# Three joints and the end of a fused two-block kernel rearranged: attention's output, the second mixer's banks and weights, the last tile in two halves

## What is computed

```
def first_block(x, ...):
    h = x
    h = h + mamba2_mixer(rms_norm(h, g_pre[0]), ...)
    k_nope, k_rope, v = mla_shared_kv(h, ...)
    h = h + mla_mixer(rms_norm(h, g_pre[1]), k_nope, k_rope, v, ...)
    return rms_norm(h, g_final)

def second_block(x, ...):
    x = x + 0.5 * swiglu(rmsnorm(x, ffn1_norm), ...)
    x = x + hybrid_mixer(rmsnorm(x, mix_norm), ...)
    x = x + 0.5 * swiglu(rmsnorm(x, ffn2_norm), ...)
    return rmsnorm(x, final_norm)
```

## Time and profile before

| what | value |
|---|---|
| median of 3 runs | 1859.54 us (1858.78 to 1861.8) |
| the profiled execution's own time | 1858.74 us |
| its span in the profile | 1856.8 us |
| TensorE busy, share of the span | 98% |
| TensorE's share of the chain that ended last | 89% |
| VectorE busy; its share of the chain | 56%; 6% |
| ScalarE busy; its share of the chain | 39%; 2% |
| mean granted clock of TensorE | 0.995 |

### The profile page before, as it was taken

One profiled execution on the slowest core, in us unless ns is written; L12 is line 12 of the kernel. 1 busy time (PEld: TensorE's weight loads), 2 busy tenths in 40 slices (PEclk: granted clock), 3 DMA queues, 4 the chain that ended last, 5 costly groups with the idle time before them and its releaser, 6 DMA issues.

```text
span 1856.8 us, 20948 instructions
## 1 busy us (share of the span) xinstructions
PE 1812.9 (98%) x8276; PEld 1458.1 (79%) x8276; DVE 1039.2 (56%) x1486; ACT 727.0 (39%) x1195; POOL 56.8 (3%) x123
## 2 busy tenths in 40 slices
PE   7899999999999999999999999999999999999997
PEld 5677777887866678888888788888888888888885
DVE  6888886566488466444433346654444544444233
ACT  4577776334366543222232333222222433232221
POOL 3000101100210000000000000000000000000000
PEclk9999999999999999999999999999999999999998
DMA  4222122322211132333333323333323223333331
GB/s 152 71 76 69 69 80 69 102 88 84 86 46 35 35 101 91 101 92 102 93 95 97 116 83 97 92 102 94 99 91 103 91 91 102 94 99 89 104 94 54
DMA packets 47041, 163.82 MB, mean 88 GB/s; under 512 B 5216, under 2 KB 5472, under 8 KB 46944
## 3 DMA queue, kind: packets, MB, share of 16 engines
q1 hardware_dynamic: 46656, 162.29, 27.8%
q10 hardware_dynamic: 288, 0.20, 0.0%
HBM read 160.37 MB, written 2.10 MB: 87 GB/s over the span
## 4 chain that ended last, share of the span: by engine, by line
PE 89%; DVE 6%; ACT 2%; issue 1%; POOL 1%; DVEq 0%; POOLq 0%; ACTq 0%
PE pb L697 27%; PE pb L699 26%; PE pb L698 26%; PE pb L782 2%; PE pb L889 2%; PE pb L894 1%; PE pb L918 1%; DVE wl L1375 1%; PE pb L1010 1%; PE pb L1012 1%; PE pb L1011 1%; ACT wr L1070 1%; DVE XL L1393 1%; PE pb L707 0%; PE pb L1020 0%
## 5 line engine op out<-in xcount | busy, mean ns | idle before, releaser
L697 PE MATMUL pb<-XR,wr 128*128 128x512 f32 x1592 | 630.6, 396 | 19.4 <-DVE XL L1393 10.6
L698 PE MATMUL pb<-XL,wr 128*128 128x512 f32 x1592 | 622.2, 391 | 0.0
L699 PE MATMUL pb<-XR,wl 128*128 128x512 f32 x1592 | 621.9, 391 | 0.0
L1375 DVE TENSOR_TENSOR wl<-raw,wr 128x1024 fp32r<-128x1024 f32 (+1 forms) x298 | 359.6, 1207 | 366.0 <-ACT wr L1070 365.2
L1070 ACT ACTIVATE wr<-raw 128x1024 fp32r<-128x1024 f32 (+1 forms) x296 | 307.1, 1038 | 308.3 <-PE pb L699 283.3
L697 PEld LDWEIGHTS pb<-XR,wr 128*128 128x128 f32 x1592 | 300.3, 189 | 86.4 <-issue 16.1
L699 PEld LDWEIGHTS pb<-XR,wl 128*128 128x128 f32 x1592 | 300.2, 189 | 63.8
L698 PEld LDWEIGHTS pb<-XL,wr 128*128 128x128 f32 x1592 | 300.6, 189 | 60.8
L1079 ACT ACTIVATE SQ<-H 128x512 f32<-128x512 f32 x42 | 26.5, 632 | 113.8 <-DVE H L1539 61.2
L697 PE MATMUL pb<-ffn1HR,wr 128*128 128x512 f32 x176 | 68.5, 389 | 0.0
L698 PE MATMUL pb<-ffn1HL,wr 128*128 128x512 f32 x176 | 68.5, 389 | 0.0
(11 more groups left out here) (316 smaller groups left out, 2227.6 us busy)
## 6 DMA issues: line engine op xcount, KB each, us to landing
raw<-in_ffn_in SPq DMA_DIRECT2D x88, 512.0 KB, 3.5
raw<-in_mix_in SPq DMA_DIRECT2D x48, 512.0 KB, 3.5
raw<-in_ssm_in SPq DMA_DIRECT2D x41, 512.0 KB, 3.3
raw<-in_ffn_out SPq DMA_DIRECT2D x32, 512.0 KB, 3.5
raw<-in_ffn_out SPq DMA_DIRECT2D x16, 384.0 KB, 3.1
raw<-in_mla_in SPq DMA_DIRECT2D x11, 512.0 KB, 3.3
raw<-in_ssm_out_a SPq DMA_DIRECT2D x8, 512.0 KB, 3.2
raw<-in_ssm_out_b SPq DMA_DIRECT2D x8, 512.0 KB, 3.2
```

What stands on the lines that cost most here:

```text
L697: e.matmul(o, r, xr, start=first, stop=False)
L698: e.matmul(o, r, xl, start=False, stop=False)
L699: return e.matmul(o, l, xr, start=False, stop=last)
L1375: e.tensor_tensor(wl[j % NS][:, 0:width(j)], raw[j % NR][:, 0:width(j)], wr[j % NS][:, 0:width(j)].bitcast(F32), ALU.subtract).then_inc(s_ ...
```

## The change

In `latents` the spread of "ck" (placing, TensorE's side, VectorE's copy) goes from `i == 4` to `i == 5`. At the end of attention the weight split is called ahead of the squares on ScalarE, the squares and folds of the last tiles stand behind ffn1's input parts, and the ring of banks leaves out bank 0. In the second mixer the second half of "vg" gets banks 0, 1, 2, 4, gates and token mixings exchange their groups of banks, and the split of the third gate's weights is called ahead of the second gelus and of the root. ffn2's ring starts with bank 1. ffn2's last output tile is computed in two halves of 256 tokens, each with its own residual, square, sums, root (two of four columns), spread and scalings; sums and spread of the first stand in the stream of the second; the stores are halves too, those of the second half's odd tiles issued by ScalarE. The diff, without new names and numbers of sessions and with the `ck` and `vg` edits that repeat left out:

```diff
@@ banks
-        if i == 4:
+        if i == 5:
             bk.place("spread ck", 7, (s_spread, spreads["ck"] + 1), (s_rk, 1))
...
-    ring = Ring([4, 5, 6, 0, 1, 2])
+    ring = Ring([4, 5, 6, 1, 2])
     for n in range(3, 8):
         bk.place(("mo", n), ring.next(), whole("mla_out", n), (s_res, 8 + n + 1))
...
-        ring = Ring([0, 1, 2, 4, 5, 6, 7])
+        ring = Ring([0, 1, 2, 4, 5, 6, 7] if f == 0 else [1, 2, 4, 5, 6, 7, 0])
...
+        if f == 1:
+            for p in range(2):
+                bk.place(("last", p), ring.next(), (s_last, p + 1), (s_res, 40 + p))
+                b = 3 if p == 0 else ring.next()
+                bk.place(("sum", p), b, (s_sums, sums_no[f"fin{p}"]), (s_sv, taken[f"fin{p}"]))
+                bk.place(("spread", p), b, (s_spread, spreads[f"fin{p}"] + 1), (s_fin, 8 * p + 8))
...
-            bk.place(("vg", hf, i), 4 + i, whole("mix_v", 4 * hf + 3), (s_vg, 4 * hf + i + 1))
+            bk.place(("vg", hf, i), ((4, 5, 6, 7), (0, 1, 2, 4))[hf][i], whole("mix_v", 4 * hf + 3),
+                     (s_vg, 4 * hf + i + 1))
...
-    ring, mring = Ring([0, 1, 2]), Ring([4, 5, 6, 7])
+    ring, mring = Ring([5, 6, 7]), Ring([0, 1, 2, 4])
@@ SP
-        for n in range(KT):
-            w.wait_ge(s_fin, n + 1)
-            e.dma_start(out[n], H[:, n, :]).then_inc(s_out, 16)
+        for p in range(2):
+            tk = slice(256 * p, 256 * p + 256)
+            for n in range(KT):
+                if p == 0 or n % 2 == 0:
+                    w.wait_ge(s_fin, 8 * p + n + 1)
+                    e.dma_start(out[n][:, tk], H[:, n, tk]).then_inc(s_out, 16)
@@ TensorE
+        def last_sums(p):
+            o = opened(("sum", p))
+            w.wait_ge(s_fold, sq.folded["fin", 6])
+            w.wait_ge(s_lastsq, p + 1)
+            for i in (2 * p, 2 * p + 1):
+                tk = slice(128 * i, 128 * i + 128)
+                e.matmul(o[:, i:i + 1], ACC[:, tk], ones[:, 0:1], start=True, stop=False)
+                m = e.matmul(o[:, i:i + 1], TB[:, tk], ones[:, 0:1], start=False, stop=True)
+            m.then_inc(s_sums, 1)
...
+        def last_tile():
+            parts = []
+            for p in range(2):
+                o = opened(("last", p))
+                tk = slice(256 * p, 256 * p + 256)
+                for t in range(FT):
+                    if p == 1 and t == 7:
+                        last_sums(0)
+                    if p == 1 and t == 17:
+                        last_spread(0)
+                    if p == 0 and t % 8 == 0:
+                        parts.append(take("ffn2_out", 21 + t // 8))
+                    r, l = parts[t // 8]
+                    w.wait_ge(s_hlo, FT + t + 1)
+                    s = slice(128 * (t % 8), 128 * (t % 8) + 128)
+                    m = three(o[:, tk], r[:, s], l[:, s], HRS[1][:, t, tk], HLS[1][:, t, tk], t == 0, t == FT - 1)
+                m.then_inc(s_last, 1)
+            last_sums(1)
+            last_spread(1)
@@ ScalarE, attention
-            for n in range(8):
-                if n:
-                    hi()
-                if n == 7:
-                    for t in range(7):
-                        w.wait_ge(s_mlo, t + 1)
-                        x_hi(t, H[:, t, :], gain2[:, t:t + 1])
+            for n in range(6):
+                hi()
                 w.wait_ge(s_res, 8 + n + 1)
-                if n == 7:
-                    w.wait_ge(*whole("mla_out", 7))
-                    x_hi(n, H[:, n, :], gain2[:, n:n + 1])
+                square(("m1", n), H[:, n, :])
+                square(("m2", n), H[:, n, :], col("g_final", n))
+            hi()
+            w.wait_ge(s_res, 15)
+            for t in range(7):
+                w.wait_ge(s_mlo, t + 1)
+                x_hi(t, H[:, t, :], gain2[:, t:t + 1])
+            w.wait_ge(s_res, 16)
+            w.wait_ge(*whole("mla_out", 7))
+            x_hi(7, H[:, 7, :], gain2[:, 7:8])
+            for n in (6, 7):
                 square(("m1", n), H[:, n, :])
                 square(("m2", n), H[:, n, :], col("g_final", n))
@@ ScalarE, second mixer
-                for k in range(4):
+                for k in range(4 + hf):
                     hi()
...
             for j in range(10):
-                if j < 8:
+                if 1 <= j < 8:
                     hi()
@@ ScalarE, end
+        for p in range(2):
+            tk = slice(256 * p, 256 * p + 256)
+            w.wait_ge(s_res, 40 + p)
+            e.activation(TB[:, tk], H[:, 7, tk], ACT.Square).then_inc(s_lastsq, 1)
+        for n in range(1, KT, 2):
+            w.wait_ge(s_fin, 8 + n + 1)
+            e.dma_start(out[n][:, 256:512], H[:, n, 256:512]).then_inc(s_out, 16)
@@ VectorE, attention
-            for n in range(8):
-                if n:
-                    lo()
-                if n == 7:
-                    for t in range(7):
-                        x_lo(4, t, H[:, t, :], gain2[:, t:t + 1])
+            for n in range(7):
                 residual(1, n, ("mo", n))
-                if n == 7:
-                    x_lo(4, n, H[:, n, :], gain2[:, n:n + 1])
-                if n >= 2:
+                lo()
+                if 2 <= n < 6:
                     fold("m1", n - 1)
                     fold("m2", n - 1)
+            for t in range(8):
+                if t == 6:
+                    residual(1, 7, ("mo", 7))
+                x_lo(4, t, H[:, t, :], gain2[:, t:t + 1])
+            for n in (5, 6):
+                fold("m1", n)
+                fold("m2", n)
@@ VectorE, end
-        fold("fin", 7)
-        root("fin")
-        w.wait_ge(*bk.full["spread fin"])
-        for n in range(KT):
-            e.scalar_tensor_tensor(out=H[:, n, :], in0=H[:, n, :], scalar=col("final_norm", n), in1=PB[3][:, :],
-                                   op0=ALU.mult, op1=ALU.mult).then_inc(s_fin, 1)
+        fold("fin", 6)
...
+        last_residual(0)
+        last_root(0)
+        last_scale(0, range(5))
+        last_residual(1)
+        last_scale(0, range(5, KT))
+        last_root(1)
+        last_scale(1, range(KT))
```

More of the change, by code:

```diff
@@ L456, in build_in @@
     spreads = {n: i for i, n in enumerate(("x", "g0", "g1", "g2", "g3", "kv", "ck", "cq", "both", "first", "mix", "f2",
-                                           "fin"))}
+                                           "fin0", "fin1"))}
     sums_no = {n: i + 1 for i, n in enumerate(("x", "g0", "g1", "g2", "g3", "kv", "ck", "cq", "m1", "m2", "mx", "f2",
-                                               "fin"))}
-    rooted = {n: (s_root, i + 1) for i, n in enumerate(("x", "kv", "first", "both", "mx", "f2", "fin"))}
+                                               "fin0", "fin1"))}
+    rooted = {n: (s_root, i + 1) for i, n in enumerate(("x", "kv", "first", "both", "mx", "f2", "fin0", "fin1"))}
     rooted.update({n: (s_groot, i + 1) for i, n in enumerate(("g0", "g1", "g2", "g3", "ck", "cq"))})
@@ L609, in place_ffn @@
                 bk.place("spread f2", 3, (s_spread, spreads["f2"] + 1), (s_rs, 5))
-        for c in range(KT):
+        for c in range(KT if f == 0 else KT - 1):
             bk.place((name, 2, c), ring.next(), whole(name + "_out", 3 * c + 2), (s_res, 16 * (f + 1) + c + 1))
+        if f == 1:
[4 more added lines that the diff above has]
+                bk.place(("spread", p), b, (s_spread, spreads[f"fin{p}"] + 1), (s_fin, 8 * p + 8))
     place_ffn(0)
@@ L638, in build_in @@
     place_ffn(1)
-    bk.place("sum fin", 3, (s_sums, sums_no["fin"]), (s_sv, taken["fin"]))
-    bk.place("spread fin", 3, (s_spread, spreads["fin"] + 1), (s_fin, 8))
     def ffn_turn(f, j):
@@ L994, in ffn, with last_spread @@
                     m.then_inc(s_unit, 1)
+        def last_sums(p):
[7 more added lines that the diff above has]
+            m.then_inc(s_sums, 1)
+        def last_spread(p):
+            o = opened(("spread", p))
+            w.wait_ge(*rooted[f"fin{p}"])
+            for i in (2 * p, 2 * p + 1):
+                m = e.transpose(o[:, 128 * i:128 * i + 128], RN[:, i:i + 1].to_broadcast([128, 128]), ident[:, :])
+            m.then_inc(s_spread, 1)
+        def last_tile():
[17 more added lines that the diff above has]
+            last_spread(1)
         def second_mixer():
@@ L1007, in second_mixer @@
                         for i in range(4):
-                            o = opened(("vg", hf, i)) if t == 0 else PB[4 + i]
+                            o = opened(("vg", hf, i)) if t == 0 else PB[bk.bank["vg", hf, i]]
                             tk = slice(128 * i, 128 * i + 128)
@@ L1049, in _ @@
         ffn(1)
-        sums("fin")
-        spread("fin")
+        last_tile()
     @block.scalar
@@ L1301, in second_mixer @@
                     w.wait_ge(*rooted["mx"])
-                    e.activation(part, PB[4 + i][:, :], ACT.Gelu_apprx_tanh, scale=RN[:, i:i + 1]).then_inc(s_vg, 1)
+                    e.activation(part, PB[bk.bank["vg", hf, i]][:, :], ACT.Gelu_apprx_tanh,
+                                 scale=RN[:, i:i + 1]).then_inc(s_vg, 1)
```

(35 more changed lines are left out.)

20 lines of the change are left out of this document (11 added, 9 removed).

## The result

The changed kernel takes 1844.36 us (median of 4 runs, 1843.38 to 1845.1), the kernel before, with a fourth run, 1859.2 (1858.78 to 1861.8). The medians are 14.8 us apart. The ratio is 0.9918 with a 95% interval of 0.9905 to 0.9932, which makes some 15.2 us less, where 12.6 were forecast. The ratio times 1859.2 is 1843.95, just beyond the low end of the range, 1844.0. The direction and the order of size were right, the size was too small. The profiled execution took 1843.38 (span 1841.6).

What follows compares the result with a forecast made beforehand. TensorE, busy 98% of the span and 89% of the chain of waits, was taken as the bound. Five terms, 1.7 + 4.5 + 4.2 + 0.7 + 1.5 = 12.6, off 1858.74 gave 1846.1, plus 0.8 for the median 1846.9 us; range 1844 to 1852.

Steps and rivals of the forecast that it cites:

- A: Latents, spread of "ck" one tile later: the transposes' wait for POOL's root goes, minus 1.7 us.
- rival 5: The latents change gives nothing, as POOL's steps meet VectorE's only in the profiled execution: 1848.6 us; chance 0.03.
- B: Attention's output to ffn1: earlier weight splits and input parts remove TensorE's waits, minus 4.5 us, bounds 2.5 and 4.5.
- the late folds: Folds of tiles 5, 6, 7 behind XL 7: last two end about 675.7 and 676.3, just in time for ffn1's sums.
- rival 1: A stall returns, from late folds before ffn1 or the fourth gate's weights; about 4.5 us lost, 1851.4; chance 0.15.
- C: Second mixer: four waits for gelu (2.9 us) and the third gate's weight wait (1.3) go, minus 4.2, bounds 2.7 and 4.3.
- D: ffn2's first tile in bank 1: no wait for the last residual, 0.3 given back at sums; minus 0.7 us.
- E: ffn2's last tile by halves: longer matmul stream, shorter chain behind it; minus 1.5 us, bounds minus 2.4 and plus 7.7.
- rivals 3 and 4: Last tile's half matmuls: bound by 0.19 weight loads, 1856.1 us, chance 0.05; or two passes in 0.49, 1895.7, chance 0.04.
- Rival 2: The tail gives nothing: the end follows the DMAs, and doubled sums and roots eat the rest; 1848.4 us; chance 0.09.

## Why the prediction fell short

**A**, forecast 1.7, measured 1.71 in the trace; no wait came back at the next weights. The wait was 1.50 to 1.54 in all six traces of a kernel without A. Two things speak against rival 5 (that the wait is rare in the timed executions): it stands in each of these traces, and the times, mostly of executions without a kept trace, differ by 13.8, of which the traces' sum with A in it gives 13.4. No run took A out by itself. The Trainium skill (SBUF — State Buffer, Who interferes with whom) says that a VectorE instruction with two SBUF inputs contends with a GpSimd one that reads SBUF. That fits with POOL's 1.11 us, but no run here took the meeting alone away.

**B**, 4.5 against 4.5 to 4.6. The step that the forecast thought nearest to failing, the late folds, had it "just in time" at the sums, and there is indeed no wait there: by the trace the last fold into ACC ended at 672.29, 0.19 ahead of the sums. So the margin was thin, and that no stall came was in part luck. Its bound below of 2.5 and rival 1 didn't come true.

**C**, 4.2 against 4.4: banks 2.9 against 3.0, gate 1.3 against 1.3. The restart of 0.24 per interruption that I put on each idle time was good to 0.1.

**D**, 0.7 against 0.55, with the wait of 0.28 for the fold as worked out (0.3). This too is the trace alone; no run took D out.

**E** is the term of the sum that was mis-sized: minus 1.5 against minus 2.2. Up to the last scaling the steps hold to 0.2: the starts 0.120 apart, so rivals 3 and 4 are refuted; the sums to the transposes 3.33 against 3.34; the transposes to the scalings 0.70 against 0.8; eight scalings 3.22 against 3.2. The step "Before, the last VectorE instruction ended at 1854.12 and the span at 1856.8, 2.7 later; I keep 2.7" failed: it is 2.15, because the last store lands 0.50 sooner after its issue. I had named 16 transfers of half the size on two queues and still kept the time of one of full size. Rival 2 saw that the end hangs on the DMAs and took it for a loss; it was a gain.

One reading in E was wrong and did no harm. The eight sums' matmuls in 1.02, my ground for a load that does not need 0.19, were put where the clock has fallen. The mean of 0.60 was of the whole stretch from 1844 to 1857; around the sums the clock was still full (the window's columns as above):

```profile
1844.00:1846.00 2.00, 1.02 (x8) 0.97 (x8) 0.69 (x5) 0.00 (x0) 0.00 (x0) 1.00 0.01 4
```

The conclusion, a load pace well under 0.19, stands without the low clock. The Trainium skill (TensorE: Matmul & The Clock Gate, Back-to-back issue gap) gives 109 ns for 256 columns; the trace has 0.120 and decides, as it did in the forecast.

**The base** is the larger part of the miss, 1.7 of the 2.5 us between the 12.6 of the forecast and the 15.1 between the two traces. The forecast took the profiled execution, put 0.8 on it for the median, and left "1 of scatter in the runs". One stretch alone, the first heads, has two levels, some 1.4 to 1.7 us apart, that go with the clock that TensorE is granted there. In the trace of before, on which the sum stood, it was low; the profile of after had it high, and by their times so had one more of its four runs. With that held, the change is worth 13.8, of which the forecast had 12.6: 0.7 lacks in E, 0.1 in A to D together, 0.25 lies outside the span, and the rest is scatter. The other 1.4 of the 15.2 were not there once the level was held, so they are no effect of the change. That the range was missed at all, by less than 0.1, hung in part on which level the first comparison met. The changed kernel's medians themselves, 1844.36 and 1844.77, lie inside it, with E as wrong as it is.

## What to carry to other kernels

Time per handover, not per instruction: the order of two engines' work, and a bank left free, was worth 4.5 us with no instruction less, and an idle time costs TensorE some 0.2 to 0.3 us over its own length. When two profiles are compared, follow the distance between the same instructions from the start; where it grows in a stretch that nobody changed, look at the granted clock, and hold that stretch still before a microsecond is credited to the change. Split a last tile as long as the matmuls' pace still nearly halves, here down to 256 columns, and at 128 no further. When the last store shrinks, the time behind the last instruction shrinks too.

## What was not expected of the hardware

The granted clock fell under a stream without a gap: with matmuls of 128 columns started 0.11 apart, TensorE stood at 1.00 from 1820 to 1830 us, at 0.73 in the next ten and at 0.50, the 1.2 GHz level, in the ten after, 10.00 of 10.00 us busy in each. The starts went from 0.11 to 0.21 apart at 1834.5, 20.8 us into the stream and half a microsecond behind half 0's eight matmuls of one column. With 256 columns, 0.12 apart and with the same eight matmuls in it, the clock stayed full through the stream; but that was over after 16.9 us, so whether 256 columns would have kept it is not shown. At the low level the quarters started 0.213 apart, and their loads were recorded with 0.33 instead of 0.19. And the level behind an idle time of 3.3 us at 78 us was low in three of the four traces that have this idle time, and high in one, with the same code; what decides between them I could not tell.
